# Moving the visits to grid attention among the input products of a two-block transformer kernel

## What is computed

```python
def second_block(x, ...):
    h = rms_norm_2(x, norm1_g)
    a, gate, q, k, v = split(h @ w_in)              # 5 x 512 columns
    conv_out = silu(layer_norm(depthwise_conv31(a * sigmoid(gate))))
    q = rms_norm_2(q per head, q_norm_g)            # 8 heads of 64
    k = rms_norm_2(k per head, k_norm_g)
    attn_out = neighbourhood_attention(q, k, v, rpb)
    x = x + concat(conv_out, attn_out) @ w_out
    h = rms_norm_2(x, norm2_g)
    return x + (silu(h @ w_gate) * (h @ w_up)) @ w_down

def neighbourhood_attention(q, k, v, rpb):          # tokens are an 8 x 64 grid
    # each query sees 8 rows x 16 columns of keys
    s = q . k_window * scale + bias
    return softmax(s) . v_window
```

## Time and profile before

| | us |
|---|---|
| median of 3 runs | 1528.15 (1526.3 to 1530.08) |
| the profiled execution | 1528.91 |
| its span | 1527.0 |
| TensorE busy | 1498.2 (98% of the span) |
| VectorE busy | 657.9 |
| GpSimd busy | 652.8 |
| ScalarE busy | 585.5 |
| mean granted clock of TensorE | 0.991 of full speed |

### The profile page before, as it was taken

One profiled execution on the slowest core, in us unless ns is written; L12 is line 12 of the kernel. 1 busy time (PEld: TensorE's weight loads), 2 busy tenths in 40 slices (PEclk: granted clock), 3 DMA queues, 4 the chain that ended last, 5 costly groups with the idle time before them and its releaser, 6 DMA issues.

```text
span 1527.0 us, 20374 instructions
## 1 busy us (share of the span) xinstructions
PE 1498.2 (98%) x7376; PEld 1188.9 (78%) x7376; DVE 657.9 (43%) x1103; ACT 585.5 (38%) x914; POOL 652.8 (43%) x303
## 2 busy tenths in 40 slices
PE   7999999999999999999999998999999999999998
PEld 6888788666678877888888886777668888888887
DVE  5312354675552547433331015888756333332001
ACT  4122333654463335323233224567654332322221
POOL 3433321564224434444444552666224444444443
PEclk9999999999999989999999999999999999999999
DMA  5532211111123322333333332421113333333333
GB/s 168 164 96 69 83 44 53 42 42 56 42 63 96 92 82 83 96 97 96 97 96 108 101 108 83 146 76 56 56 56 97 96 96 96 96 96 97 111 97 110
DMA packets 40893, 135.04 MB, mean 88 GB/s; under 512 B 4464, under 2 KB 8816, under 8 KB 40576
## 3 DMA queue, kind: packets, MB, share of 16 engines
q1 hardware_dynamic: 39504, 130.56, 28.7%
q10 hardware_dynamic: 1328, 3.64, 0.8%
HBM read 132.09 MB, written 2.10 MB: 88 GB/s over the span
## 4 chain that ended last, share of the span: by engine, by line
PE 93%; DVE 4%; ACT 1%; issue 1%; DMA 0%; POOL 0%; DVEq 0%; SPq 0%; ACTq 0%
PE bank L1060 21%; PE bank L1061 20%; PE bank L1062 20%; PE bank L1089 3%; PE bank L1091 3%; PE bank L1090 3%; PE bank L1362 3%; PE bank L1364 2%; PE bank L1363 2%; PE bank L1266 2%; PE bank L1285 1%; PE bank L1300 1%; PE bank L1417 1%; DVE ssum L1619 1%; DVE bank L2025 1%
## 5 line engine op out<-in xcount | busy, mean ns | idle before, releaser
L426 POOL TENSOR_TENSOR wL<-raw,wH 128x1024 fp32r<-128x1024 f32 x235 | 574.4, 2444 | 824.1 <-ACT wH L516 647.4
L516 ACT ACTIVATE wH<-raw 128x1024 fp32r<-128x1024 f32 x209 | 221.4, 1059 | 618.7 <-PE bank L1062 573.7
L1060 PE MATMUL bank<-aH,wH 128*128 128x512 f32 x1016 | 398.9, 393 | 2.4 <-DVE aL L1684 1.1
L1061 PE MATMUL bank<-aL,wH 128*128 128x512 f32 x1016 | 396.0, 390 | 0.0
L1062 PE MATMUL bank<-aH,wL 128*128 128x512 f32 x1016 | 395.9, 390 | 0.0
L1060 PEld LDWEIGHTS bank<-aH,wH 128*128 128x128 f32 x1016 | 191.1, 188 | 48.0 <-issue 4.1
L1062 PEld LDWEIGHTS bank<-aH,wL 128*128 128x128 f32 x1016 | 191.1, 188 | 39.9
L1061 PEld LDWEIGHTS bank<-aL,wH 128*128 128x128 f32 x1016 | 191.2, 188 | 39.8 <-issue 0.7
L1060 PE MATMUL bank<-fH,wH 128*128 128x512 f32 x352 | 137.2, 390 | 0.0
L1062 PE MATMUL bank<-fH,wL 128*128 128x512 f32 x352 | 137.0, 389 | 0.0
L1061 PE MATMUL bank<-fL,wH 128*128 128x512 f32 x352 | 137.0, 389 | 0.0
(11 more groups left out here) (299 smaller groups left out, 1871.5 us busy)
## 6 DMA issues: line engine op xcount, KB each, us to landing
raw<-in_w SPq DMA_DIRECT2D x235, 512.0 KB, 3.5
bmk<-in_bias SPq DMA_DIRECT2D x6, 512.0 KB, 4.9
pj<-in_x SPq DMA_DIRECT2D x4, 512.0 KB, 6.5
out_x<-z2T SPq DMA_DIRECT2D x8, 256.0 KB, 3.5
ct<-in_ct ACTq DMA_DIRECT2D x3, 384.0 KB, 3.1
w1k<-in_w1k ACTq DMA_DIRECT2D x1, 1024.0 KB, 6.9
w1v<-in_w1v ACTq DMA_DIRECT2D x1, 1024.0 KB, 5.1
pv<-in_pv ACTq DMA_DIRECT2D x1, 128.5 KB, 4.7
```

Source lines behind the costliest of these rows:

```text
L426: pool.tensor_tensor(wL[:, c_slot, :], raw[:, c_slot, :], wH[:, c_slot, :].bitcast(F32), ALU.subtract).then_inc(sem("w_lo"), 1)
L516: act.activation(wH[:, s, :], raw[:, s, :], ACT.Copy).then_inc(sem("w_hi"), 1)
L1060: pe.matmul(bank[:], hi, H[:, ka, :], start=(k == 0), stop=False)
L1061: pe.matmul(bank[:], hi, L[:, ka, :], start=False, stop=False)
```

## The change

The change adds and removes no instruction. It moves some on three engines.

- TensorE, input products: `turned` goes from k = 3 and `values` from k = 6 to k = 1, so that scores, value turns, turned and values stand in one visit, in this order. The column sum of slot 19 goes from k = 2 to k = 4.
- TensorE, output projection: `values` goes from the fourth product of a slot to the third, where `turned` stands.
- ScalarE: the scaling `over_sums` goes ahead of its two taps.
- VectorE: the first group of taps in a slot is at most two (before, half of what is left), then comes the reciprocal, then the copy of the turned probabilities, then all other taps. Before, the copy stood ahead of the reciprocal.

```diff
--- before.py
+++ after.py
@@ -940,10 +940,10 @@
                     act.wait_ge(sem("conv_in"), 2)
                     act.activation(yT[:, 3, :], up[:, 3, 0:S], ACT.Identity, scale=pv[:, w:w + 1], bias=vec("dw_bias", 3))\
                         .then_inc(sem("conv_mul"), 1)
+                if t in STEP_AT:
+                    over_sums(STEP_AT[t])
                 if 4 <= t < 4 + TAPS // 2:
                     taps(2 * t - 7, 2)
-                if t in STEP_AT:
-                    over_sums(STEP_AT[t])
                 if t in SUMS_AT:
                     head_roots(SUMS_AT[t])
 
@@ -1483,20 +1483,20 @@
                             value_turns(VALUES_AT[t], 0)
                         if t - 1 in VALUES_AT:
                             value_turns(VALUES_AT[t - 1], 1)
-                    if k == 2 and t == NT2 - 1:
+                        if t - 1 in STEP_AT:
+                            turned(STEP_AT[t - 1])
+                        if t - 2 in STEP_AT:
+                            values(STEP_AT[t - 2])
+                    if k == 4 and t == NT2 - 1:
                         pe.wait_ge(sem("ln_add"), 3)
                         pe.wait_ge(sem("conv_out"), 3)
                         pe.matmul(B[7][:], ones, ssum[:], start=True, stop=True).then_inc(sem("sum_ready"), 1)
                     if k == 2 and t in SPREAD_AT:
                         head_spread(SPREAD_AT[t], 0)
-                    if k == 3 and t - 1 in STEP_AT:
-                        turned(STEP_AT[t - 1])
                     if k == 4 and t in SUMS_AT:
                         head_sums(SUMS_AT[t])
                     if k == 5 and t in SPREAD_AT:
                         head_spread(SPREAD_AT[t], 1)
-                    if k == 6 and t - 2 in STEP_AT:
-                        values(STEP_AT[t - 2])
                     mm = block_product(B[(p.t0 + t) % NBANK if t < 4 else t % 2], (p.c0 + t) % 2, k, aH[:, k, :], aL[:, k, :], k == 0, k == KD - 1)
                 mm.then_inc(sem("chunk_done"), 1)
 
@@ -1506,7 +1506,7 @@
                 slot, b = NT2 + n // 4, n % 4
                 if b == 2 and slot - 1 in STEP_AT:
                     turned(STEP_AT[slot - 1])
-                if b == 3 and slot - 2 in STEP_AT and slot < 28:
+                if b == 2 and slot - 2 in STEP_AT and slot < 28:
                     values(STEP_AT[slot - 2])
                 if slot == 28 and b == 0:
                     values(15)
@@ -2087,12 +2087,12 @@
                     masked_max(STEP_AT[t])
                 if t in SPREAD_AT:
                     normed(SPREAD_AT[t], 0)
-                taps(left // 2)
-                left -= left // 2
+                taps(min(left, 2))
+                left -= min(left, 2)
+                if t in STEP_AT:
+                    over_sums(STEP_AT[t])
                 if t - 1 in STEP_AT:
                     copied(STEP_AT[t - 1])
-                if t in STEP_AT:
-                    over_sums(STEP_AT[t])
                 if t == 15:
                     dve.wait_ge(sem("conv_out"), 2)
                     dve.wait_ge(sem("sum_ready"), 4)
```

## The result

The changed kernel takes 1534.38 us (median of 6 runs, 1532.84 to 1538.77), the kernel before 1528.47 beside it (6 runs, 1526.3 to 1531.44). The ratio is 1.004, with a 95% interval from 1.0027 to 1.0053: slower by 0.4%. The profiled execution took 1533.58 us with a span of 1531.6, against 1528.91 and 1527.0 before. The time lies inside the range of the prediction, 2.2 us above its point. "Within 0.3%" had the largest chance there (0.60), and the result is just on the other side of that bound.

A forecast was written before the change was run, and what follows sets the result against it. TensorE was taken to bound the kernel (93% of the span). Savings -3.7, stalls +6.1 and clock +1.7 gave +4.1 on 1527.0, so 1531.1, or 1532.2 us against the median; range 1526.5 to 1536.0.

The forecast's parts named there:

- TensorE sets the end: Whole kernel: TensorE's chain, 93% of the span, ends last; a wait costs its full length if TensorE waits.
- Values wait for L896 in slots 15 and 10: TensorE stops at the moved values until ScalarE's copy L896 is done: 4.6 us in slot 15, 1.3 in slot 10.
- The pushes: Delays on ScalarE and VectorE from slots 12 to 14 make slot 15's copy later, raising its stall from 3.4 to 4.6.
- The merges save 1.6: Input products, slots 9 to 19: joining small work in one visit saves longer steps at seams, 1.6 us (1.3 to 1.95).
- The projection saves 0.6: Output projection, slots 20 to 27: values moved to the third product save 0.6 us, range 0.3 to 1.0.
- The column sum, -1.1: Slot 19: moving the column sum to k = 4 covers its wait for L909; 1.1 us saved, 1.5 with head sums.
- The spread in slot 12 is late and pushes VectorE by up to 1: Slot 12: first spread of the roots stands behind turned and values, 1.0 us later, pushing VectorE back by up to 1.
- Nothing on TensorE waits for GpSimd: GpSimd adds ScalarE's taps up to 1 us later, but no TensorE work here waits for its low halves.
- The clock, +1.7: Slot 15's stall brings one more stretch at 1.2 GHz, costing 1.7 us, range 0 to 3.4.
- (a): Rival: values don't stall in slots 10 and 15; -3.5 us, 1524.7; chance 8%.
- (b): Rival: stalls of 3.4 and 0.6 us without pushes, and the clock holds; +0.5 us, 1528.7; chance 22%.
- (c): Rival: slot 15's stall and lower clock feed each other, slot 19's column sum waits again; +7.3 us, 1535.4; chance 15%.

The follow-up runs named there:

- the stop of slot 15 alone: Kernel before with only the values of step 4 moved from k = 6 to k = 1 of slot 15: 1532.63 us, ratio 1.003.
- TensorE's half alone: Changed kernel's TensorE order with ScalarE and VectorE ordered as in the kernel before: 1533.23 us, ratio 1.0027.

## Why the prediction came out as it did

**The main mechanism was right, its sum was right by compensation.** The steps in order:

- *TensorE sets the end.* Right: nearly every microsecond that TensorE waited more is in the span.
- *Values wait for L896 in slots 15 and 10.* Right in place and cause, shown by removal (5.2 of 5.9 us) and alone (+4.0). Slot 15 was put at 4.6, range 3.4 to 5.0, and measured 3.8. The pushes were there, and larger than the 1.2 in the sum: the copy ended 1.9 later, 1.3 of it by the order on ScalarE and VectorE. But the value turns in slot 15 also came 1.35 later than before, counted from the first scores, and the seams took 0.25 more; this takes from the wait and not from the loss: it is the same time, lost earlier. Slot 10 was put at 1.3 and measured 0.4, for the same reason. Its copy L896 ended 0.7 later, counted from the first scores (15.76 for 15.09), nearly the 0.8 that was foreseen; but TensorE's value turns came 0.8 later too (14.47 for 13.69), behind the turned of slot 9 and the product that waited for GpSimd. The step that failed here is that TensorE would be on time at the values.
- *The merges save 1.6.* Mis-sized: 0.7. The failed step is "their step in could be 0 or 0.09". In slot 11 turned to values took 0.53 where the sum had 0.36, and value turns to turned 0.49 where it had 0.42. That is 0.24 in a slot that was to save 0.26. The trace before had one seam between small pieces (scores to transposes, 0.06 more), and that is the cheapest of the three.
- *The projection saves 0.6.* Wrong: +0.4. The same failed step explains why nothing is saved. Of the 0.4 that is lost, some 0.27 lie in slot 20 at the token sums; the rest stays open.
- *The column sum, -1.1.* Right: -1.08, its step is the plain 0.23 now. The other 0.4 of that term was misread: the wait at L1373 in the earlier trace rows lies in slot 6, outside the moved instructions. Some 0.2 came at slot 16.
- *The spread in slot 12 is late and pushes VectorE by up to 1.* Half right: the push was seen (1.24), but only as a push on the copy L896. That TensorE's own scores need L2065 was left out: 1.8 us, the largest term missed. "In slots 13 to 14, 18 and all later ones VS is a slot old and nothing waits" looked at VS alone.
- *Nothing on TensorE waits for GpSimd.* Wrong by 0.6: ScalarE's taps come later, GpSimd's additions L483 wait for them, and the low half L426 stands behind these. For slot 10 it started 1.8 later, not "up to 1 us", and its slack before was 1.2 (it ended at 1003.87, the product started at 1005.11).
- *The clock, +1.7.* The stretch behind the stop came as foreseen (1052 to 1056). The one at 1060 did not, so the difference is 0. The prediction named this case in the range, not in the sum.

Of the terms, -3.7 became -1.6 (merges 0.7, column sum 1.1, head sums 0.2, less 0.4), +6.1 became +4.3, +1.7 became 0, and +2.4 of waits came from places that the prediction said held none. Together +5.1 for +4.1.

**The rivals.** (a), no stop, fell. (b), a short stop and a clock that holds, is wrong in its reason: the pushes did come, and the clock behind the stop fell. But its prices, 4.2 for the stops and nothing for the clock, are nearer to what was measured (4.3 and 0) than the 6.1 and 1.7 of the forecast case. What carried the loss past its +0.5 are the missed waits and the merges. (c), in which the column sum waits again, did not happen in the changed kernel, but in two kernels beside it (2.4 and 3.5 us), with 10.2 and 3.4 us of the lower clock behind it. Its place was right, its mechanism not: not a long chain of late taps, but one VectorE instruction that starts inside one of GpSimd's. The changed kernel missed that by 0.5 us (L2109 at 1085.74, L426 at 1086.21).

**The chances.** The point was 2.2 us low of the measured median. With the two missed waits in the sum (+2.4) and the merges at 0.7, the point would have been above the bound for slower, and "slower" the likeliest case.

## What to carry to other kernels

When an instruction is moved ahead on an engine that never waits, list for each of its inputs who makes it and where that maker stands in its own order, and then do the same for every instruction that the moved one is now ahead of: here the second list (the spread, then the norm, then the next scores) held 1.8 us. A merge of small matmuls saves only the long steps at its seams, and a seam between two kinds of small work can be as dear as the seam to the products; read both before putting a number on it. Where VectorE adds two SBUF tiles and GpSimd works in long instructions, look at the distance between their starts, above all where VectorE waits for the very instruction behind which GpSimd starts the long one: an exchange elsewhere that moves one of them by a microsecond cost 2 us there. And when two traces are compared, count from a common point: here half a microsecond of offset hid that both a copy and its reader had moved.

## What the runs showed of the hardware that was not expected

- Four transposes between products cost 0.36 from start to start, and 0.42 with scores ahead of them; with other transposes behind them it was 0.50, and 0.52 with the small matmuls of the values behind them (slot 11 above).
- A VectorE addition of 128 x 512 from two SBUF tiles took 0.69 us alone and 2.76 to 2.79 where it started 0.14 to 0.15 us after a GpSimd instruction of 2.4 us; it ended 0.54 after GpSimd's end both times. It costs the rest of the other instruction, not a share.
- The clock: stops of 3.7 and 3.5 us were each followed by 3.4 us at 1.2 GHz (after, and the stop of slot 15 alone); one of 2.4 us in slot 15 (TensorE's half alone) by none in that execution; with one of 2.4 us at the column sum (the copy moved earlier) came 10.2 us, and with one of 3.5 us there (ScalarE's order alone) 3.4. The clock fell 1.2, 0.5 and 1.3 us after TensorE had come back in the changed kernel, slot 15 alone and ScalarE's order alone, and 0.5 before it came back where the copy was moved earlier. The stretch of 3.4 us behind the head sums of slot 16 came in some profiled executions and not in others with the same instructions up to there. So a single profiled execution can differ by 1.7 us for no reason of its order. What decides between these cases was not settled.
